# A four-stage float32 encoder kernel: the first bank set of each output projection between the last head's steps, and all memory attention of the first layer in one stretch

## The reference, cut to what matters

```python
def memory_attention(mq, mem_k, mem_v):            # 4 heads, 256 memory tokens
    sc = jnp.einsum('bthd,blhd->bhtl', qh, mem_k) * (MEM_HEAD_DIM ** -0.5)
    p = jax.nn.softmax(sc, axis=-1)
    return jnp.einsum('bhtl,blhd->bthd', p, mem_v).reshape(b, s, MEM_WIDTH)

def retention_layer(a, mem_k, mem_v, w_in, w_out, gn_g, gn_b, decay):
    q, k, v, g, mq = jnp.split(a @ w_in, ...)
    qh, kh = rotary(q), rotary(k)                  # per head
    y = forward_scan(qh, kh, vh) + backward_scan(qh, kh, vh)
    y = silu(g) * group_norm(y)
    return jnp.concatenate([y, memory_attention(mq, mem_k, mem_v)], axis=-1) @ w_out
...
for i in range(DEPTH):
    h = h + rms_norm(mixer(rms_norm(h)), ...)      # retention_layer, then na_layer
    h = h + rms_norm((silu(gate) * up) @ ffn_w_out[i], ...)
```

## Time and profile before

| | |
|---|---|
| median of 3 runs | 2473.19 us (2467.92 to 2474.19) |
| profiled execution | 2470.92 us, its span 2469.1 us |
| busy share of the span | PE 95%, PEld 78%, DVE 50%, ACT 38%, POOL 42% |
| PE share of the chain that ended last | 82% |
| first memory attention with 32 pieces | 62.7 to 128.3 us |
| last head of the first layer with 8 rows | 414.5 to 473.9 us |
| last head pair of the second layer | 1661.4 to 1696.9 us |

### The profile page before, as it was taken

One profiled execution on the slowest core, in us unless ns is written; L12 is line 12 of the kernel. 1 busy time (PEld: TensorE's weight loads), 2 busy tenths in 40 slices (PEclk: granted clock), 3 DMA queues, 4 the chain that ended last, 5 costly groups with the idle time before them and its releaser, 6 DMA issues.

```text
span 2469.1 us, 30580 instructions
## 1 busy us (share of the span) xinstructions
PE 2347.4 (95%) x11048; PEld 1929.8 (78%) x11048; DVE 1244.8 (50%) x2203; ACT 935.1 (38%) x1853; POOL 1046.3 (42%) x793
## 2 busy tenths in 40 slices
PE   7999998798999999999989999999889999999998
PEld 6788887676778888788867788877767888887886
DVE  5544444636644444576854333345366344345767
ACT  5412112346233333344644444445452332333443
POOL 4132222267977777100342222212588777770001
PEclk9999999999999999999999999999999999999999
DMA  6111112243343232733521111123423333228334
GB/s 209 35 52 43 60 44 86 69 156 100 109 152 103 98 120 94 298 94 95 163 84 43 40 40 41 41 69 111 149 100 127 125 119 111 90 94 307 94 98 149
DMA packets 101923, 259.99 MB, mean 105 GB/s; under 512 B 21759, under 2 KB 22030, under 8 KB 99726
## 3 DMA queue, kind: packets, MB, share of 16 engines
q1 hardware_dynamic: 101774, 258.04, 31.5%
HBM read 193.25 MB, written 64.77 MB: 104 GB/s over the span
## 4 chain that ended last, share of the span: by engine, by line
PE 82%; DVE 5%; issue 4%; ACT 3%; POOL 3%; DMA 2%; SPq 0%; ACTq 0%; POOLq 0%; DVEq 0%
PE PS L1940 23%; PE PS L1942 23%; PE PS L1941 23%; PE PS L2172 3%; PE PS L2401 2%; PE PS L2182 2%; DMA stage<-in_wpack 1%; PE PS L2206 1%; PE PS L2279 1%; DMA SRAW<-hidden_scratch 1%; POOL rstd L723 1%; POOL msq L722 1%; PE PS L1963 1%; PE PS L2357 1%; DVE Hb L1443 0%
## 5 line engine op out<-in xcount | busy, mean ns | idle before, releaser
L1940 PE MATMUL PS<-AOP,OPS 128*128 128x512 f32 x1232 | 483.6, 393 | 26.8 <-ACT Hb L1020 16.1
L1942 PE MATMUL PS<-AOP,OPS 128*128 128x512 f32 x1232 | 482.2, 391 | 0.0
L1941 PE MATMUL PS<-AOP,OPS 128*128 128x512 f32 x1232 | 482.1, 391 | 0.0
L710 POOL TENSOR_TENSOR wlo<-stage,whi 128x1024 fp32r<-128x1024 f32 x82 | 197.3, 2409 | 539.5 <-ACT whi L925 539.1
L1940 PE MATMUL PS<-aT,whi 128*128 128x512 f32 (+1 forms) x768 | 335.8, 437 | 5.7 <-DVE aT L1410 4.2
L1942 PE MATMUL PS<-aT,wlo 128*128 128x512 f32 (+1 forms) x768 | 298.4, 388 | 0.0
L1941 PE MATMUL PS<-aT,whi 128*128 128x512 f32 (+1 forms) x768 | 297.7, 388 | 0.0
L1940 PEld LDWEIGHTS PS<-AOP,OPS 128*128 128x128 f32 x1232 | 233.0, 189 | 80.5 <-POOL OPS L755 24.2
L755 POOL TENSOR_TENSOR OPS<-TW,OPS 128x512 fp32r<-128x512 f32 x176 | 237.3, 1354 | 89.6 <-ACT OPS L1007 87.8
L1007 ACT ACTIVATE OPS<-TW 128x512 fp32r<-128x512 f32 x176 | 110.4, 631 | 426.0 <-POOL TW L779 380.2
L1942 PEld LDWEIGHTS PS<-AOP,OPS 128*128 128x128 f32 x1232 | 232.9, 189 | 48.8
(11 more groups left out here) (196 smaller groups left out, 4042.7 us busy)
## 6 DMA issues: line engine op xcount, KB each, us to landing
stage<-in_w SPq DMA_DIRECT2D x98, 512.0 KB, 3.6
stage<-in_wpack SPq DMA_DIRECT2D x82, 512.0 KB, 3.6
hidden_scratch<-HT SPq DMA_DIRECT2D x154, 256.0 KB, 2.1
SRAW<-hidden_scratch SPq DMA_DIRECT2D x154, 256.0 KB, 2.7
BW<-in_w SPq DMA_DIRECT2D x16, 1024.0 KB, 11.0
h_scratch<-Hb SPq DMA_DIRECT2D x24, 512.0 KB, 2.9
Hb<-h_scratch SPq DMA_DIRECT2D x24, 512.0 KB, 5.8
cat_scratch<-OC SPq DMA_DIRECT2D x13, 512.0 KB, 3.0
```

Of the source, the lines that this page charges most:

```text
L710: pool.tensor_tensor(wlo[:, slot, :], stage[:, slot, :], whi[:, slot, :].bitcast(F32), ALU.subtract)\
L1940: pe.matmul(dst, stat[0], mov[0], start=start, stop=False, skip_group_check=onto)
L1941: pe.matmul(dst, stat[0], mov[1], start=False, stop=False, skip_group_check=onto)
L1942: return pe.matmul(dst, stat[1], mov[0], start=False, stop=stop, skip_group_check=onto)
```

## The change

- The first layer's 16 rows of memory attention all stand in the first stretch (`RUN_A0 = (0, 16, 0, 0)`, 19 steps) with the same 32 pieces. `RUN_B0` is gone. The memory heads' outputs become slices 0 and 1 of the concatenation, the retention heads slices 2 to 7 (the weight rows are ordered to match), and only the last head writes `catf` directly.
- The two rotations of head 0 are cut in four parts, one for a step (`parts`).
- In the first layer the units of heads 1 to 5 use banks 4 to 7 and the steps' tiles banks 0 to 3 (`unit_bank`); before it was the other way round.
- Between the last head's steps stand slices of the first set of the output projection (`out_rows`). The second layer has 24 of its 32 tile groups between the rows of the last pair.
- Outputs of heads come back in two halves of 256 KB for each slice (`cat_back(l, th, tiles)`), the first token half ahead of the last head's store. `cat_split` of the first slices moves forward on ACT and DVE.
- SP loads the residual tiles and the gain row (`before_out(0)`) after the memory attention instead of before `out_phase(0)`.

The core of the diff:

```diff
-        RUN_A0 = (0, 8, 0, 0)
-        RUN_B0 = (8, 8, 1, 7)
+        RUN_A0 = (0, 16, 0, 0)
         RUN_A1 = (16, 16, 0, 8)
...
-        DIRECT = (6, 7, 15)
+        DIRECT = (7, 15)
...
+        def unit_bank(n):
+
+            return 2 * (n % 2) + (4 if U_RETH + 4 <= n < U_OUT0 else 0)
+
         def banks(r):
 
-            return (r % 2, 2, 3) if RUN_B0[0] <= r < R_END[0] else (4 + r % 2, 6, 7)
+            return 4 + r % 2, 6, 7
...
-                sp.wait_ge(oc_rdy, 8 * l + 8)
+                sp.wait_ge(oc_rdy, 16 if l else 2)
...
-            def cat_back(l, tiles):
-
+            def cat_back(l, th, tiles):
+
+                cols = slice(HALF * th, HALF * th + HALF)
                 sp.wait_ge(*USED[U_OUT[l] - 1])
                 for k in tiles:
                     sp.wait_ge(oc_st[k % 2], stored(8 * l + k))
-                    sp.dma_start(catf[:, k, :], cat_dram[l, k, :, :]).then_inc(cat_ld[k], 16)
+                    sp.dma_start(catf[:, k, cols], cat_dram[l, k, :, cols]).then_inc(cat_ld[th][k], 16)
 
...
             sp.wait_ge(t_done, turned(2))
             sp.dma_start(dconst[:, :, :], decay_consts[:, 0:6 * P].rearrange("p (a c) -> p a c", a=6)).then_inc(c_ld, 16)
+            load_units(U_RETH + 6)
+            store_cat(0)
+            load_units(U_RETH + 7)
+            store_cat(1)
+            before_out(0)
             load_units(U_RETH + 4 + 5)
-            store_cat(0)
             for h in range(1, RH):
                 load_units(U_RETH + 4 * h + 4 + 5)
-                store_cat(h)
+                if h == RH - 1:
+                    cat_back(0, 0, range(KD - 2))
+                store_cat(h + 1)
             load_units(U_OUT0 + 5)
-            cat_back(0, range(RH))
-            before_out(0)
+            cat_back(0, 1, range(KD - 2))
+            for th in range(2):
+                cat_back(0, th, [KD - 2])
             out_phase(0)
             ffn(0)
...
-                if h < RH:
-                    his(n + 3)
+                his(n + 3)
+                if h == RH:
+                    cat_split(0, range(1))
...
-                        mem_step(RUN_B0, t)
-                    cat_split(0, range(2))
+                    cat_split(0, range(2, KD - 2))
+                    his(U_OUT0 + 4)
+                    cat_split(0, range(KD - 2, KD - 1))
+                    his(U_OUT0 + 5)
 
                 act.wait_ge(y_tr, h)
                 for b in range(2):
...
 
-            def rotate(n, dst):
+            def rotate(n, dst, parts=range(4)):
 
                 dve.wait_ge(*USED[n])
-                for th in range(2):
+                for part in parts:
+                    th = part // 2
                     cols = slice(HALF * th, HALF * th + HALF)
-                    src = PS[:, 2 * (n % 2) + th, :]
-                    dve.tensor_tensor(dst[:, cols], src, ropeC[:, cols], ALU.mult)
-                    dve.tensor_tensor(rtmp[0:64, :], src[64:128, :], ropeS[64:128, cols], ALU.mult)
-                    link(dve.tensor_tensor(rtmp[64:128, :], src[0:64, :], ropeS[0:64, cols], ALU.mult))
-                    ins = dve.tensor_tensor(dst[:, cols], dst[:, cols], rtmp[:, :], ALU.add)
-                    if th == 0:
-                        link(ins)
-                ins.then_inc(ev_dve, 1)
-
-                dve.wait_ge(*EV[n])
+                    src = PS[:, unit_bank(n) + th, :]
+                    if part % 2 == 0:
+                        dve.tensor_tensor(dst[:, cols], src, ropeC[:, cols], ALU.mult)
+                        link(dve.tensor_tensor(rtmp[0:64, :], src[64:128, :], ropeS[64:128, cols], ALU.mult))
+                    else:
+                        link(dve.tensor_tensor(rtmp[64:128, :], src[0:64, :], ropeS[0:64, cols], ALU.mult))
+                        ins = dve.tensor_tensor(dst[:, cols], dst[:, cols], rtmp[:, :], ALU.add)
+                        if th == 0:
...
+                cat_split(0, range(2))
                 values(h)
-                for t in range(3):
-                    mem_step(RUN_B0, t)
-                scan(h, lambda c: mem_step(RUN_B0, 3 + c // 2) if c in (1, 3, 5) else None)
-                mem_step(RUN_B0, 6)
-                group_norm(h, lambda: mem_step(RUN_B0, 7))
-                mem_step(RUN_B0, 8)
-                cat_split(0, range(2))
+                cat_split(0, range(2, 4))
+                scan(h)
+                cat_split(0, range(4, KD - 2))
+                group_norm(h)
+                cat_split(0, range(KD - 2, KD - 1))
                 gated_values(h)
-                for t in range(9, steps(RUN_B0) + 1):
...
+                    if hp == HP and t in (2, 5, 8, 11, 14):
+                        cat_split(1, [(t + 1) // 3])
             out_phase(1)
...
+            def out_rows(l, st, k, tiles=range(TT), free=None):
+
+                n, th, fh = U_OUT[l] + 4 * st + k // 2, st // 2, st % 2
+                if k % 2 == 0:
+                    pe.wait_ge(w_lo, n + 1)
+                pe.wait_ge(cat_lo, 16 * l + 8 * th + k + 1)
+                for i in tiles:
+                    if k == 0:
+                        for s, v in free(i):
+                            pe.wait_ge(s, v)
+                    rows, f = slice(i * P, (i + 1) * P), slice(HALF * (k % 2), HALF * (k % 2) + HALF)
+                    ins = three(PS[:, (D0[l] if fh else 4 - D0[l]) + i, :], (catT[:, th, 0, k, rows], catT[:, th, 1, k, rows]),
+                                (whi[:, w_slot(n), f], wlo[:, w_slot(n), f]), k == 0, k == KD - 1)
+                    if k == KD - 1:
+                        ins.then_inc(y_done, 1)
+                if k % 2 and tiles[-1] == TT - 1 and USED[n][0] is w_used:
                     ins.then_inc(w_used, 1)
...
-                for st, free in enumerate((first, second, third)):
+                for k in range(6, KD):
+                    out_rows(l, 0, k, range(2 if l == 0 and k == 6 else 0, TT))
+                for st, free in ((1, second), (2, third)):
                     for u in range(4):
...
 
+            low, high = range(2), range(2, TT)
             chunk_scores(RH)
-            for u in range(1, 4):
-                pe.wait_ge(*EV[U_OUT0 - u])
-            for t in range(3):
-                mem_step(RUN_B0, t)
+            out_rows(0, 0, 0, free=first_set_free(0))
+            out_rows(0, 0, 1, low)
             chunk_states(RH)
-            for t in range(3, 6):
-                mem_step(RUN_B0, t)
+            out_rows(0, 0, 1, high)
+            out_rows(0, 0, 2)
             chunk_outputs(RH)
-            for t in range(6, 9):
-                mem_step(RUN_B0, t)
+            for k in range(3, 5):
+                out_rows(0, 0, k)
             turn_outputs(RH)
-            for t in range(9, steps(RUN_B0)):
-                mem_step(RUN_B0, t)
+            out_rows(0, 0, 5)
+            out_rows(0, 0, 6, low)
...
                     pieces(hp, pieces_at(t, PIECES, ROWS, EARLY))
+                    if hp == HP and t:
+                        for m in range(24 * (t - 1) // (LAST - 1), 24 * t // (LAST - 1)):
+                            out_rows(1, 0, m // TT, range(m % TT, m % TT + 1), first_set_free(1))
...
```

More of the change, by code:

```diff
@@ L223, in trunk_program @@
         oc_st = [sem(f"oc_st{i}") for i in range(2)]
-        cat_ld = [sem(f"cat_ld{k}") for k in range(KD)]
+        cat_ld = [[sem(f"cat_ld{th}_{k}") for k in range(KD)] for th in range(2)]
         cat_hi, cat_lo = sem("cat_hi"), sem("cat_lo")
@@ L688, in _ @@
                     load_bias(hp + 1)
+                if hp == HP - 1:
+                    cat_back(1, 0, range(KD - 2))
                 store_cat(9 + hp)
             load_units(U_OUT1 + 5)
-            cat_back(1, range(KD - 1))
+            cat_back(1, 1, range(KD - 2))
+            for th in range(2):
+                cat_back(1, th, [KD - 2])
             before_out(1)
@@ L1371, in _ @@
                 r0 = R_ROW + ROWS * (hp - 1)
+                if hp == HP:
+                    his(U_OUT1 + 3)
+                    cat_split(1, range(1))
                 for t in range(LAST):
@@ L1460, in out_phase @@
                 s, t = 2 * l, 4 * l + 3
[L1461 removed]
+                cat_split(l, range(KD - 1 if l == 0 else KD - 2, 2 * KD))
                 dve.wait_ge(g_ld, 16 * (s + 1))
@@ L1850, in _ @@
                 decays(t)
-                for u in units_done(t, 4 * KD, steps(RUN_A0)):
-                    if u < 2:
-                        rotate(U_RETH + u, (qT[:, 0, :], kT[:, :])[u])
+                for ago in range(4):
+                    for u in units_done(t - ago, 4 * KD, steps(RUN_A0)):
+                        if u < 2:
+                            rotate(U_RETH + u, (qT[:, 0, :], kT[:, :])[u], (ago,))
             for h in range(1, RH + 1):
@@ L2022, in first_two, with out_unit, first_set_free @@
                     project(n + 1, k, (1,))
[L2024 to L2041 removed]
+            def out_rows(l, st, k, tiles=range(TT), free=None):
[13 more added lines that the diff above has]
```

(8 more changed lines are left out.)

115 lines of the change are left out of this document (52 added, 63 removed).

## The result

The changed kernel takes 2449.78 us (median of 4 runs, 2445.93 to 2452.77), the kernel before 2471.32: a ratio of 0.9911 with a 95% interval of 0.9898 to 0.9924, so 0.9% faster and clear of the noise. Forecast were 2448 and a range of 2439 to 2457. Run once more in a later session (e9), it took 2451.24 against 2473.44, ratio 0.9914 (0.9898 to 0.993). The profiled executions differ by 25.0 us (2470.92 and 2445.93), where the sum of the prediction was 24.9. That this sum fits so closely is partly chance, as the rows show.

The account below looks back on a forecast made before the run. PE bounds the kernel, busy 95% of the span, so time can come only from its waits and half-clock matmuls. Terms 19.6 - 38.0 - 6.5 = -24.9 take the profiled 2470.9 us to 2446.0, the median to 2448; range 2439 to 2457.

Parts of the forecast that it names:

- First stretch: First layer's first memory attention with 8 rows added: 84.9 us against 65.3, so +19.6 us.
- the loop: First stretch, steps 4 to 9: DVE-ACT round with decay table, 5.9 us with a rotation part; 5.6 us of waits and half clock.
- Case 2: First stretch: POOL's four low-half subtractions hold DVE up to 2.4 us each inside the loop; +8.7, 2457 us; chance 0.07.
- Case 6: First stretch: the closed loop holds for all 19 steps, not five; +47 us there, slower overall; chance 0.03.
- Heads 1 to 5: First layer's heads 1 to 5: other banks, same order and waits; change of 0.
- Last head: First layer's last head to the first set's end: 82.8 us falls to 44.8, so -38.0 us.
- The 0.9 for late slices and clock: First layer's last head: 0.9 us added for late slices and for half clock after the two waits.
- Rival 3: First layer's last head: slices land late, ACT's copy of k waits, steps start at half clock; +8, 2456 us; chance 0.10.
- Last pair: Second layer's last head pair to the set's end: 57.4 us falls to 50.9, so -6.5 us.
- The 3.0 of waits: Second layer's last pair: late start from ACT's splits 1.3 us, a last copy, and a 0.7 us wait; 3.0 us.
- the second rival: First stretch: POOL's low-half subtractions hold DVE for their whole length through the shared port; +8.7, 2457 us; chance 0.07.
- rival 4: Second layer: gains nothing, as splits on DVE and ACT break the rows' round; 2454.5 us; chance 0.06.

Follow-up runs that it names:

- e2: Changed kernel with the six decay tables of the first memory attention in steps 13 to 18 instead of 4 to 9; 2448.45 us, ratio 0.9897.
- e4: Changed kernel with the slices of the concatenated heads loaded as whole tiles instead of halves; 2455.37 us, ratio 0.9925.
- e7: Changed kernel with the first layer's first projection set behind the last head's steps, not between them; 2469.29 us, ratio 0.9981.
- e6: Changed kernel with e5's line, a weight unit's split moved behind step 5 and slice 6 split in step 17, second layer's last pair; 2448.92 us, ratio 0.9896.
- e5: Changed kernel with two second-layer weight units requested before the loads that wait for the last pair's output; 2450.03 us, ratio 0.9897.
- e10: Changed kernel with e2's late tables, e6's edits, and three pieces of head 5's last unit held back with ACT's order changed; 2437.95 us, ratio 0.9859.
- e3: Changed kernel with the first stretch's two rotations done whole in the step where their unit ends, not in parts; 2461.04 us, ratio 0.9952.
- e1: Changed kernel with the second layer's fill undone and its splits back where they were; 2453.37 us, ratio 0.9919.

## Why the prediction was right, and where not

**First stretch, forecast +19.6, right in size and mechanism.** 84.9 us, and e2 shows the loop by taking it away. Two sizes in it were off and cancelled. The loop cost 4.9 us, where I had 5.6, and 0.9 more for POOL. In the first profile the 4.9 are all waits, with a clock of 1.00; in e9 they are 3.4 of waits and the rest half clock, nearer to what I wrote, at the same length. The work was 1.6 us more than 78.4: e2, with none of those waits, still has a stretch of about 79.7. Case 2 is out here: of POOL's four subtractions one held DVE, by 1.4 us (the scaling of a maximum at 134.15 took 1.58 us, not 0.17), and PE waited for none. Case 6 (slower) is refuted: the round without the table is covered.

**Heads 1 to 5, forecast 0.** From 147.6 to 433.9, 286.3 us; before, from 128.25 to 414.47, 286.2.

**Last head, forecast -38.0, measured -38.9.** Each wait came within 0.2 us of its term. The 0.9 for late slices and clock wasn't needed. Rival 3 is refuted by the profile and by e4: its low half is ready at 440.5 us and PE's first group starts at 442.95, and whole tiles did no worse. e7 divides the gain: 13 to 14 us are waits and half clock filled by the set; the other 25 are the 8 rows that left (17.6) and the waits that went with them.

**Last pair, forecast -6.5, measured 0: the step that failed.** It was written as "47.9 + 3.0 = 50.9", counted to the set's end. The 3.0 of waits was the first fault: the set's end came at 55.3 us, and at 53.7 in e2, e7 and e9, where less ran at half clock. The start alone took 2.62 us and half clock for it. About 1 us of that is ACT's order, which I had; the other 1.7 are new: POOL's subtraction for the weight unit, now split there, held DVE's split of slice 0 until it ended. This is the second rival's mechanism, which I had looked for in the first stretch only. The Trainium skill's page "SBUF — State Buffer", section "SBUF: two separate sides", tells of that exclusive lock, for a DVE operation with two inputs in SBUF too, as the split is; the rows under e6 agree, with 2.41 against 0.69 us. The second fault was to stop at the set's end. What is late next is the load of the set's second successor unit, which waits for the same last output as before while its cover shrank from 21 to 7 us: 1.4 to 2.4 us of wait, and in three of seven profiles some 1.6 us of half clock more. e5 takes this wait away and shows its worth in the stretch from slice 7 on: 50.0 us instead of 52.3 to 54.8. In the first layer the change moved those loads of h forward, so there it didn't arise. e6 and e10 mend both faults, and the pair then gives 5.0 to 6.1 us in D (e6 and e10 against before). So rival 4, at 0.06, was what happened in this layer, and for a reason that it didn't name.

**The sum.** By A to D the change gives 19 us in the first profile (22 in e9), and the medians differ by 21.5 and 22.2. I forecast 24.9. The 25.0 between the two profiled executions is 19 and a low N. That the median came within 2 us of the 2448 has luck in it too: the gain was 3.4 us less than forecast, and the kernel before, whose median I took as 2473.19, has 2471.32 with a fourth run.

## What to carry to other kernels

When a block of work is laid into waits, the end of that block comes sooner after the last input; look which loads and splits had counted on the block as their cover, and request them first. A gain counted "to the set's end" is none until the next unit's weights are there.

Before a closed loop over several engines is accepted, look for work in it that is not due yet: the decay tables cost 5 us in steps 4 to 9 and nothing in steps 13 to 18, ahead of head 1. An operation in pieces is worth most where such a loop has no slack (8 us here).

Changes of 5 us can't be read from this kernel's total. Compare stretches between fixed rows, and let one stretch that no edit touches tell how much the rest varies by itself.

## What the runs showed of the hardware

The granted clock did not fall at every wait. After 2.15 us of waiting (changed kernel, first stretch) it stayed at full speed, 2.4 GHz; after 2.16 us at the same place of the same code (e9) it fell, to 0.72 in the mean of the window shown above, so part of that window ran at 1.2 GHz. After 4.42 and 4.73 us (e3) products took 2.04 us instead of 1.03, half clock. After the same wait of 3.08 us ahead of the last head, in the same code, the eight transposes took 1.94 us in some profiles (changed, e4, e5) and 1.06 in others; of these, e2, e3 and e6 had the slow matmuls a little later, in the scores (2.9 to 3.2 us instead of 2.05), and e1, e7 and e9 had none. From the transposes to the set's first group it was 4.1 us in e1 and e9, 4.9 in the changed kernel and 6.3 in e4. So a wait of that size has no fixed price: with it B lies between 83.7 and 86.0 us in runs without a new wait there, and D of the changed code between 100.5 and 104.7.

Without touching them, the stretches N differ by up to 11 us between executions of thirteen kernels, twice the size of most single edits here.
